# Two transformer blocks in fp32 on one core: the seams between stages by halves of 512 columns, weight splits moved behind the norms, accumulators opened by two columns, the last stage tile by tile

## What is computed

```
h = h + rmsnorm(mix, g_post_mix);  u = rmsnorm(h, g_pre_ffn)               # seam 1: out-projection -> FFN 1
h = h + rmsnorm(square(relu(u @ w_ff1)) @ w_ff2, g_post_ffn)
u = rms_norm(h, ln_pre_mix)                                                # seam 2: FFN 1 -> block 2's projections
h = h + rms_norm(merged @ w_out, ln_post_mix);  f = rms_norm(h, ln_pre_ffn)   # seam 3 -> FFN 2
h = h + rms_norm((silu(f @ w_gate) * (f @ w_up)) @ w_down, ln_post_ffn)    # seam 4 -> last stage
h = h + sigmoid(h @ w_ple_gate) * rms_norm(p @ w_ple, ln_ple)
```

## Time and profile before

| | us |
|---|---|
| runs of the kernel | 1061.08, 1063.28, 1063.31 (median 1063.28) |
| span of the profiled execution, first to last instruction | 1062.7 |
| PE busy | 933.3 (88%) |
| DVE busy | 580.4 (55%) |
| ACT busy | 515.9 (49%) |
| mean granted TensorE clock, share of full | 0.949 |

### The profile page before, as it was taken

The page is one execution under the profiler, slowest core; times in us unless marked ns, Lnnn a source line. Parts: engine busy times, 40 slices in busy tenths (PEclk is TensorE's granted clock), DMA queues, the critical chain, the costliest instruction groups (busy, mean ns, idle before and its releaser), DMA issues.

```text
span 1062.7 us, 16705 instructions
## 1 busy us (share of the span) xinstructions
PE 933.3 (88%) x6486; PEld 856.1 (81%) x6486; DVE 580.4 (55%) x842; ACT 515.9 (49%) x859; POOL 139.2 (13%) x131
## 2 busy tenths in 40 slices
PE   1598769999999789988699898998988999999967
PEld 1596548999897788988688888888976799999946
DVE  1376554555556555558463737363656455555454
ACT  2458453444445544555636464636336444444442
POOL 4000021000000000007555545300000000000000
PEclk9699889999999889999899999999989899999969
DMA  9643227565556244444122222222554465555601
GB/s 191 210 160 119 79 57 158 188 197 193 169 192 198 75 131 152 124 152 144 62 73 84 76 80 79 80 80 80 180 188 134 142 192 170 194 197 170 231 34 39
DMA packets 106876, 144.88 MB, mean 136 GB/s; under 512 B 3104, under 2 KB 94368, under 8 KB 106704
## 3 DMA queue, kind: packets, MB, share of 16 engines
q1 hardware_dynamic: 104304, 137.37, 40.7%
q0 software_dynamic: 2208, 6.25, 2.8%
q10 hardware_dynamic: 320, 0.66, 0.2%
HBM read 143.22 MB, written 1.05 MB: 136 GB/s over the span
## 4 chain that ended last, share of the span: by engine, by line
PE 73%; DVE 11%; ACT 9%; DMA 3%; issue 3%; POOL 1%; SPq 0%; ACTq 0%; DVEq 0%; POOLq 0%
PE ps L1497 13%; PE ps L1499 13%; PE ps L1498 13%; PE ps L1503 8%; PE ps L1505 8%; PE ps L1504 8%; DVE wl L1044 3%; DMA w_raw<-in_w_in_dram 3%; ACT wh L601 3%; PE ps L1799 2%; PE ps L1810 1%; DVE xTl L1072 1%; PE ps L1688 1%; PE ps L1814 1%; PE ps L1631 1%
## 5 line engine op out<-in xcount | busy, mean ns | idle before, releaser
L1044 DVE TENSOR_TENSOR wl<-w_raw,wh 128x1024 fp32r<-128x1024 f32 x258 | 322.8, 1256 | 354.8 <-ACT wh L601 354.2
L1497 PE MATMUL ps<-xTh,wh 128*128 128x256 f32 (+1 forms) x1160 | 339.2, 292 | 29.3 <-DVE xTl L1072 20.3
L601 ACT ACTIVATE wh<-w_raw 128x1024 fp32r<-128x1024 f32 x258 | 270.5, 1052 | 133.1 <-PE ps L1505 85.7
L1498 PE MATMUL ps<-xTl,wh 128*128 128x256 f32 (+1 forms) x1160 | 329.2, 284 | 0.0
L1499 PE MATMUL ps<-xTh,wl 128*128 128x256 f32 (+1 forms) x1160 | 328.9, 284 | 0.0
L1497 PEld LDWEIGHTS ps<-xTh,wh 128*128 128x128 f32 x1160 | 222.4, 192 | 34.1 <-DVE xTl L1072 20.7
L1498 PEld LDWEIGHTS ps<-xTl,wh 128*128 128x128 f32 x1160 | 221.3, 191 | 2.6 <-issue 1.7
L1499 PEld LDWEIGHTS ps<-xTh,wl 128*128 128x128 f32 x1160 | 222.2, 192 | 0.0
L1503 PE MATMUL ps<-wh,y 128*128 128x512 f32 x224 | 88.9, 397 | 4.0 <-DVE y L1452 4.0
L1505 PE MATMUL ps<-wh,y 128*128 128x512 f32 x224 | 88.6, 395 | 0.0
L1504 PE MATMUL ps<-wl,y 128*128 128x512 f32 x224 | 88.1, 393 | 0.0
(11 more groups left out here) (331 smaller groups left out, 1337.7 us busy)
## 6 DMA issues: line engine op xcount, KB each, us to landing
w_raw<-in_w_in_dram SPq DMA_DIRECT2D x43, 1024.0 KB, 5.2
w_raw<-in_w_ff_dram SPq DMA_DIRECT2D x32, 1024.0 KB, 5.4
w_raw<-in_w_ffn_gate_dram SPq DMA_DIRECT2D x11, 1024.0 KB, 5.3
w_raw<-in_w_ffn_up_dram SPq DMA_DIRECT2D x11, 1024.0 KB, 5.4
w_raw<-in_w_ffn_down_dram SPq DMA_DIRECT2D x11, 1024.0 KB, 4.9
w_raw<-in_w_out_dram SPq DMA_DIRECT2D x8, 1024.0 KB, 4.8
w_raw<-in_w_proj_a_dram SPq DMA_DIRECT2D x4, 1024.0 KB, 5.0
w_raw<-in_w_proj_b_dram SPq DMA_DIRECT2D x4, 1024.0 KB, 4.9
```

The lines of the kernel that those rows point to most:

```text
L601: act.activation(split_view(wh, pu % UNITS, layout), raw_unit(SLOT[p], j, layout), ACT.Copy).then_inc(w_hi, 1)
L1044: TT(split_view(wl, pu % UNITS, layout), raw_unit(SLOT[p], j, layout), split_view(wh, pu % UNITS, layout).bitcast(F32), ALU.subtract).then ...
L1497: mm(out, wh_, xh, start=first, stop=False)
L1498: mm(out, wh_, xl, start=False, stop=False)
```

## The change

1. Sums of squares, scalings and additions are done by halves of 512 columns, in new statistics cells `nst`; each half of `acc`, h and u is signalled on its own (`rows_done`, `h_ready`, `u_ready`), and PE transposes a piece when its half is ready. The first half's mean is put into the root's bias by an `Identity` on one column.
2. The order in the seams is written out anew. In seam 1 ACT and DVE do tile 0's second norm ahead of tile 1's first. The `hi` of the seam's units stand where ACT's queue has a place for them, and most `lo` come behind the four pieces.
3. The first unit of the new stage begins when three of the four pieces are there (`first_unit`; in `slice_up` by two waits).
4. `open_acc` multiplies two columns a bank, not 512, and comes behind the first two (FFN 1) or four (FFN 2) units.
5. Seam 2: the 16-column product comes behind the first unit. Seam 3: PE transposes tile 0 between the two PLE units; the copy out of PSUM is done by tile.
6. The last stage's first four units go tile by tile; the last tile's half is signalled when done.

```diff
+            def square_half(src, half, at):
+                cols_ = slice(half * 512, half * 512 + 512)
+                ch.link(act.activation(junk[:, cols_], src, ACT.Square, accum_out=nst[:, at + half:at + half + 1]))
+                if half == 0:
+                    ch.mark(act.activation(nst[:, at + 2:at + 3], nst[:, at:at + 1], ACT.Identity, bias=eps[:, 0:1], scale=1.0 / D))
+            def sums_root(n, t, last_unit):
...
+                        act.wait_ge(rows_done, 3 * n + 2 * t + half + 1)
+                    square_half(acc[:, 2 * t + half, :], half, 4 * t)
+                root_of(4 * t)
+            def rows_root(n, t):
+                for half in range(2):
+                    act.wait_ge(h_ready, 4 * n + 2 * t + half + 1)
+                    square_half(h[:, t, half * 512:half * 512 + 512], half, 8 + 4 * t)
+                root_of(8 + 4 * t)
...
-            turn(0, 21, range(22, 26))
+            act.preload_act_table(ACT.Sqrt)
+            sums_root(0, 0, 21)
+            hi(22)
+            hi(23)
+            rows_root(0, 0)
+            sums_root(0, 1, 21)
+            piece_hi(0)
+            piece_hi(1)
+            rows_root(0, 1)
+            hi(24)
+            piece_hi(2)
+            piece_hi(3)
+            hi(25)
...
-            turn(1, F + 63, (F + 66, F + 67))
+            act.preload_act_table(ACT.Sqrt)
+            sums_root(1, 0, F + 63)
+            sums_root(1, 1, F + 63)
+            hi(F + 66)
+            rows_root(1, 0)
+            rows_root(1, 1)
+            for n in range(4):
+                piece_hi(n)
+            hi(F + 67)
...
-            turn(2, 2 * P_OUT2 + 7, (2 * P_FF2, 2 * P_FF2 + 1), ple_rows)
+            sums_root(2, 0, 2 * P_OUT2 + 7)
+            sums_root(2, 1, 2 * P_OUT2 + 7)
+            hi(2 * P_FF2)
+            rows_root(2, 0)
+            hi(2 * P_FF2 + 1)
+            rows_root(2, 1)
+            piece_hi(0)
+            piece_hi(1)
+            ple_rows(0)
+            piece_hi(2)
+            piece_hi(3)
+            ple_rows(1)
+            hi(2 * P_FF2 + 2)
+            hi(2 * P_FF2 + 3)
...
+            def add_rows(g, t):
...
+                for half in range(2):
+                    cols_ = slice(half * 512, half * 512 + 512)
+                    ins = STT(u[:, t, cols_], acc[:, 2 * t + half, :], nst[:, 4 * t + 3:4 * t + 4], gain[:, g % 2, cols_], ALU.mult, ALU.mult)
...
+                    TT(h[:, t, cols_], h[:, t, cols_], u[:, t, cols_], ALU.add).then_inc(h_ready, 1)
...
-            turn(1, range(22, 26))
+            add_rows(1, 0)
+            lo(22)
+            norm_rows(1, 0)
+            add_rows(1, 1)
+            piece_lo(0)
+            piece_lo(1)
+            norm_rows(1, 1)
+            piece_lo(2)
+            piece_lo(3)
+            for n in range(23, 26):
+                lo(n)
...
-            turn(5, (2 * P_FF2, 2 * P_FF2 + 1))
-            lo(2 * P_FF2 + 2)
-            lo(2 * P_FF2 + 3)
+            add_rows(5, 0)
+            add_rows(5, 1)
+            norm_rows(5, 0)
+            lo(2 * P_FF2)
+            norm_rows(5, 1)
+            for n in range(4):
+                piece_lo(n)
+            for n in range(1, 4):
+                lo(2 * P_FF2 + n)
...
-                    mm(acc[:, q, :], zero_r[:, :], junk0, start=True, stop=False, skip_group_check=True)
-
-            junk0 = cst[:, 0:512]
+                    mm(acc[:, q, 0:2], zero_r[:, :], junk0, start=True, stop=False, skip_group_check=True)
+
+            junk0 = ident[:, 0:2]
+            first_unit(fm_steps(F, xTh, xTl, 0, S))
+            run(fm_steps(F + 1, xTh, xTl, 0, S))
             open_acc()
-            ffn1_up(F)
...
-            for k in range(2):
-                acc_unit(2 * P_PLE + k, pT_h[:, k, :], pT_l[:, k, :], k == 0, k == 1, into=high)
-            transposes(u, u_ready, 7)
-            pieces_ready()
+            acc_unit(2 * P_PLE, pT_h[:, 0, :], pT_l[:, 0, :], True, False, into=high)
+            transposes(u, u_ready, 11, range(2))
+            acc_unit(2 * P_PLE + 1, pT_h[:, 1, :], pT_l[:, 1, :], False, True, into=high)
+            transposes(u, u_ready, 11, range(2, 4))
...
-            transposes(h, h_ready, 6)
-            pieces_ready()
-            for k in range(4):
-                acc_unit(2 * P_PGATE + k, xTh[:, k, 0:S], xTl[:, k, 0:S], k == 0, False)
+            transposes(h, h_ready, 12)
+            for t in range(NT):
+                pe.wait_ge(ut_lo, pieces[0] - 2 + 2 * t)
+                for k in range(4):
...
```

More of the change, by code:

```diff
@@ L612, in _ @@
             pieces = [1]
[L614 to L629, removed]
-                    else:
[L631 to L643, removed]
@@ L1059, in _, with inverse @@
             roots, pieces = [0], [1]
-            def inverse(at, n=P):
+            def inverse(at, n=P, of=st):
                 roots[0] += 1
                 dve.wait_ge(stat, roots[0])
[L1065 to L1084, removed]
+                link(dve.reciprocal(of[0:n, at:at + 1], of[0:n, at:at + 1]))
@@ L1112, in _ @@
                ALU.subtract).then_inc(ut_lo, 1)
-            pieces_lo(META)
+            for n in range(4):
+                piece_lo(n, META)
             lo(4)
@@ L1239, in _ @@
             acc_units(F + 60)
-            turn(3, (F + 66, F + 67))
+            add_rows(3, 0)
+            add_rows(3, 1)
+            norm_rows(3, 0)
+            norm_rows(3, 1)
+            for n in range(4):
+                piece_lo(n)
+            lo(F + 66)
+            lo(F + 67)
             dve.wait_ge(ab_hi, 1)
@@ L1464, in _ @@
                 hid2_mul(F2 + 56 + 6 * n, 0, 0, n + 9)
-            turn(7, (F2 + 68, F2 + 69), norm=False)
+            add_rows(7, 0)
+            add_rows(7, 1)
+            for n in range(4):
+                piece_lo(n)
+            lo(F2 + 68)
+            lo(F2 + 69)
             for n in range(4):
@@ L1587, in _ @@
             last.then_inc(ut_ps, 1)
-            transposes(u, u_ready, 1)
+            for n in range(4):
+                if n % 2 == 0:
+                    pe.wait_ge(u_ready, n // 2 + 2)
+                transpose_piece(u, n)
             pieces_ready()
@@ L1701, in _ @@
             acc_tail((F + 62, F + 63), [(hid_h[:, 1, j, :], hid_l[:, 1, j, :]) for j in range(2)])
-            transposes(u, u_ready, 5)
-            pieces_ready()
-            pe.wait_ge(ab_lo, 1)
-            for k in range(KC):
-                last = three(ma[0:16, 0:S], ab_h[:, k, :], ab_l[:, k, :], xTh[:, k, 0:S], xTl[:, k, 0:S], k == 0, k == KC - 1)
-            last.then_inc(ab_ps, 1)
+            transposes(u, u_ready, 7)
             M, G = 2 * P_MOBA, 2 * P_GDN
@@ L1719, in _ @@
             steps = pair_steps("ffffff" + "tt", M, 0, 0)
-            for _ in range(16):
+            first_unit(steps)
+            pe.wait_ge(ab_lo, 1)
+            for k in range(KC):
+                last = three(ma[0:16, 0:S], ab_h[:, k, :], ab_l[:, k, :], xTh[:, k, 0:S], xTl[:, k, 0:S], k == 0, k == KC - 1)
+            last.then_inc(ab_ps, 1)
+            for _ in range(8):
                 next(steps)
@@ L1917, in slice_up @@
                     for k in range(KC):
+                        if need is None and stride == 0 and j == 0 and k % 4 == 0:
+                            pe.wait_ge(ut_lo, pieces[0] - 1 + k // 4)
                         last = three(banks[j], a[:, k, :], b[:, k, :], xTh[:, k, 0:S], xTl[:, k, 0:S], k == 0, k == KC - 1)
```

122 lines of the change are left out of this document (80 added, 42 removed).

## The result

The changed kernel takes 1045.79 us (median of 4 runs, 1045.07 to 1048.64) against 1063.3 us of the kernel before beside it: ratio 0.9843, 95% interval 0.9824 to 0.9861. A later comparison on another chip gave 1046.04 against 1064.25, ratio 0.983 (0.9809 to 0.9851). The prediction said 1048.0, between 1043.0 and 1054.0. The profiled execution is the longest of the four, 1048.64 us with a span of 1046.7.

What follows compares the result with a forecast made beforehand. PE's work was taken as the bound, except where PE stands at the four seams. Terms of -5.4, -2.0, -3.2 and -4.7 sum to -15.3 on a span of 1062.7; median forecast 1048.0, range 1043.0 to 1054.0.

Steps and rivals of the forecast that it cites:

- the sums: Four seams: walked chains put the first useful work earlier by 8.5, 2.3, 4.6 and 3.4 us.
- the two estimated prices: Seam chains by halves: squares on ACT 1.65 us a tile for 1.15, scaling and adding on DVE 3.0 for 2.66.
- the prediction's last part: Signs in the trace: first useful product 9.8, 10.0, 5.6 us behind seams 1, 2, 4's last matmul; seam 3's gate 14.8.
- the small one: Two-column opening of the accumulators, seams 1 and 3: eight passes cost 0.9 us, bounds 0.4 and 1.7 in seam 1.
- The clock: PE restarts behind seams: half clock falls on useful work, costing 2.2 us in seam 1, 0.3 in 2, 0.5 in 3.
- The rival that the clock returns sooner: PE's restarts: half clock as short as in seam 2, or absent; about 4 us more gained, 1044; chance 0.15.
- the terms of the clock and of the last stage: Half clock costs 2.2, 0.3, 0.5 us in seams 1 to 3; seam 4: start -3.4, clock -0.7, end -0.6.
- the new wait between the PLE units: Seam 3: PE stands 3.7 us for tile 0's u, yet the gate starts 4.6 us earlier; seam sum -3.2.
- halving as such moves a chain by only some tenths: Seam chains: 512-column halves cost little beyond 0.1 us an operation; the gain is in what leaves the chain.
- the prediction's rule on DVE: Weighed for DVE: latency per instruction, 0.157 us; about six added ones a chain cost 0.4 us more a seam, 1049.6.
- the prediction's 0.02 to 0.1: DVE: cost in us of each instruction added by halving, taken from profile rows.
- the rival that ends slower: FFN stages: late weight loads, not PE, set the pace; +7.4 us, 1070.7; chance 0.03.

Runs made afterwards that it cites:

- the second profile: The changed kernel, nothing altered, profiled again; its span is 18.6 us less than before the change, against 16.0 less in the first profile.
- the openings alone: Kernel before the change, with its two accumulator openings at their old places but 2 columns wide, not 512: 1059.81 us, ratio 0.9953.
- the combination: Changed kernel with whole tiles, both PLE units ahead of seam 3's transposes, and zero matmuls in PE's gaps except seam 3: 1035.79 us, ratio 0.9743.

## Why the prediction was right

**The chains.** All four starts came within 0.3 us of the sums (seam 3 within 0.4 in the second profile): 10.2 for 155.25 - 145.07 = 10.2; 10.6 for 10.4; 14.9 for 15.1; 6.0 for 6.0 (the marks of the prediction's last part count from the end of the last matmul, 0.4 us later). They rest on durations from rows and on following every instruction of ACT and DVE in its new order; the two estimated prices hold: ACT's 1.65 us a tile by halves is 1.61 in the profile (145.90 to 147.51), and DVE's 3.0 for scaling and adding a tile is 2.98 with the reciprocal ahead of it (803.77 to 806.75).

**The openings.** Predicted 0.9 for the small one, from the row of eight passes; measured 0.81. The columns don't set its pace: passes of 2 columns take 0.10 us each and those of 128 columns 0.11, while those of 512 take 0.38. That it is the weights that do was the prediction's estimate; no run tells them from another fixed cost of a pass.

**The clock.** It was put at +2.2, +0.3 and +0.5 us behind the first three seams. With the opening taken off, seam 1 shows +1.8 and +1.5 in the two profiles, seam 3 +0.2 and -0.3. The rule of the Trainium skill that the throttled clock is the default ("TensorE: Matmul & The Clock Gate", Part 1) spoke against the change; the trace agrees in kind, with 0.50 behind seams 1 and 2 and 0.66 over seam 3's PLE unit in the first profile, and the openings alone show its price: of 8.0 us saved at the starts 2.8 were given back. The rival that the clock returns sooner did not come about in seam 1: from 155.55 to about 160.1 the products start 0.21 us apart. In seam 2 it came about in the second profile (346.80 above) and not in the first, so that the +0.3 there was met by neither; that the terms of the clock and of the last stage came out near their sum is in part luck of the execution.

**Seam 3.** The prediction saw the new wait between the PLE units (3.7 us; 3.71 in the profile) and still a gain, because ACT's copies and splits, which had been last, left the chain. That holds. What it did not ask is what the old order of those two units would give with the other edits kept: 2.7 us more at the start, 3.8 in the time.

**Halving.** That "halving as such moves a chain by only some tenths" is what the runs showed, with a minus: whole tiles are shorter by 0.3 us over the four seams at the clock as it comes, and by 1.8 with the clock held. By the prediction's rule on DVE (the Trainium skill, "VectorE: DVE Perf Modes", TRN2 errata section: each instruction adds its latency, 0.157 us) two more instructions a tile would cost 0.31; scaling and adding a tile take 2.78 us by halves (141.88 to 144.66 in the changed kernel) and 2.46 whole (141.71 to 144.17 in the whole-tile kernel), 0.32. The trace agrees with the page there, and the prediction's 0.02 to 0.1 was too low for them: it came from instructions of which none waits for the one before. Its sum didn't suffer, since the walk through the seams had 3.0 for 2.66. A norm by halves adds one instruction, of which neither half waits for the other, and 0.13 us (809.91 to 811.24 for 805.69 to 806.89 in seam 3).

**The size.** Predicted -15.3 on the span, measured -16.0 and -18.6. The terms that moved between the two are above all the lengths behind seams 2 and 4. Of what was taken apart, the openings as narrow ones at their old place give 5.3 us, the moved splits 5.3 and the last stage by tiles 1.3; the rest, 4 to 7 us by the one profile or the other (the three-piece start, ACT's order in seam 3, the end, less what halving and the new place of the PLE unit cost), was not undone by itself, and parts measured one at a time need not add up.

**Weights.** Nothing waited for them: the feed-forward stages' loads are missing from the changed kernel's list of waits for DMA, and the rival that ends slower had no place.

## What to carry to other kernels

Walk a seam instruction by instruction from measured durations, and put into the chain only what the next stage waits for; weight splits of later units belong behind it, and count for what they cost only where the engine would not have stood idle. Splitting a step in halves pays only where a follower would otherwise stand, and each half costs an instruction; here whole tiles were faster. Before filling a wait by moving real work out of a place where it was free, look whether TensorE then stands: here the PLE unit in its old place kept both the time and the clock. And where TensorE must wait, matmuls of zeros into a free bank or added to an open accumulator keep its clock, worth 8.9 us of 1046.

## What the hardware showed that was not expected

- The clock at a restart can be bought: matmuls of zeros in PE's gaps, 106 more PE instructions in the page's count, took the mean granted clock of the profiled executions from 0.957 to 0.985 and the median time down by 8.9 us, while no useful start came more than 0.3 us later behind its old stage. A seam can lose the clock without a long wait in it: with gaps of 0.41, 1.44 and 1.06 us the gate of the combination started at 1.2 GHz, and with 0.40, 1.44 and 1.06 so did that of the kernel with whole tiles and PLE units first; in the kernel with the PLE units first alone, gaps of 0.99, 1.34 and 1.23 us left it at 2.4 GHz. These are one execution each, and no rule on the length of gaps follows: seam 2 of the changed kernel restarted at either clock behind the same gaps.
- The clock differs between executions of one program, away from the seams too: from 25 to 50 us it is 0.62 or 0.57 in the two profiles of the changed kernel and 1.00 in that with the zeros, which has none there, and the last matmul ahead of seam 1 comes at 145.35, 144.93 and 145.73, so that this stretch doesn't depend on it. The long stage behind seam 2 differs in both: 0.97 and 0.98, 456.4 and 453.8 us. The changed kernel's times scatter by 3.6 and 5.1 us within its two groups of runs. How much of that is the clock isn't shown, but it is a reason to read changes of 1 or 2 us at the starts in a profile rather than in the times.
- An opening of 512 columns in fp32 is eight passes of 0.38 us, not sixteen at the pace of the split products.
